# Fourier mixer of a two-block transformer kernel: projection folded into the feature tables, token transform in even and odd halves

## The reference, cut to what matters

```python
def fourier_mixer(hf, fnet_w, fnet_b):
    b, s, _ = hf.shape
    g = hf.reshape(b, s, FNET_GROUPS, FNET_GROUP_DIM).astype(jnp.float32)
    mixed = jnp.real(jnp.fft.fft2(g, axes=(1, 3), norm="ortho")).astype(hf.dtype)
    out = jnp.einsum('bsgc,gcd->bsgd', mixed, fnet_w) + fnet_b[None, None]
    return out.reshape(b, s, FNET_WIDTH)

def first_block(x, ...):
    x = x + 0.5 * swiglu(rms_norm(x, ffn1_norm), ffn1_w_gate, ffn1_w_up, ffn1_w_down)
    h = rms_norm(x, mix_norm)
    u = h @ w_in
    f_out = fourier_mixer(u[..., :o0], fnet_w, fnet_b)
    a_out = gqa_attention(u[..., o0:o1], u[..., o1:o2], u[..., o2:], q_norm, k_norm)
    x = x + jnp.concatenate([f_out, a_out], axis=-1) @ w_out
    ...
```

## Time and profile before

| what | value |
|---|---|
| median of 3 runs | 1262.18 us (1260.85 to 1262.86) |
| the profiled execution's own time | 1260.8 us |
| span of its trace | 1259.0 us |
| PE busy | 1243.9 us (99%) |
| PEld busy | 1104.9 us (88%) |
| DVE busy | 925.3 us (73%) |
| ACT busy | 657.5 us (52%) |
| mean granted TensorE clock | 0.995 |

### The profile page before, as it was taken

One profiled execution on the slowest core, in us unless ns is written; L12 is line 12 of the kernel. 1 busy time (PEld: TensorE's weight loads), 2 busy tenths in 40 slices (PEclk: granted clock), 3 DMA queues, 4 the chain that ended last, 5 costly groups with the idle time before them and its releaser, 6 DMA issues.

```text
span 1259.0 us, 18129 instructions
## 1 busy us (share of the span) xinstructions
PE 1243.9 (99%) x7458; PEld 1104.9 (88%) x7458; DVE 925.3 (73%) x1295; ACT 657.5 (52%) x867; POOL 30.9 (2%) x23
## 2 busy tenths in 40 slices
PE   8999999999999999999999999999999999999997
PEld 7888889878888888888888888889998888888886
DVE  7887856587877855988658777659977657877743
ACT  6655534364655543546546555545555445555432
POOL 0000000000000000440000000000000000000000
PEclk9999999999999999999999999999999999999998
DMA  8465754134555663555336555753435534555550
GB/s 312 174 227 186 230 190 164 68 106 163 200 179 189 200 235 128 173 197 173 136 137 228 201 179 190 226 176 135 168 135 182 186 134 139 200 197 192 192 185 34
DMA packets 51426, 221.74 MB, mean 176 GB/s; under 512 B 4464, under 2 KB 5776, under 8 KB 30864
## 3 DMA queue, kind: packets, MB, share of 16 engines
q1 hardware_dynamic: 51200, 220.52, 50.9%
q10 hardware_dynamic: 144, 0.07, 0.0%
HBM read 219.52 MB, written 1.05 MB: 175 GB/s over the span
## 4 chain that ended last, share of the span: by engine, by line
PE 91%; DVE 6%; ACT 1%; DMA 1%; issue 1%; SPq 0%; DVEq 0%; ACTq 0%
PE bank L405 48%; PE bank L435 21%; PE bank L409 7%; PE bank L426 4%; PE bank L474 2%; DVE wt L1153 2%; PE bank L685 2%; PE bank L713 2%; PE bank L451 1%; PE bank L477 1%; DVE xn L1162 1%; DVE x L1167 1%; PE bank L510 1%; DVE x L1168 1%; PE bank L456 1%; DMA x<-x_t 1%
## 5 line engine op out<-in xcount | busy, mean ns | idle before, releaser
L1153 DVE TENSOR_TENSOR wt<-raw,wt 128x2048 fp32r<-128x2048 f32 x202 | 464.1, 2299 | 69.0 <-ACT wt L831 68.6
L831 ACT ACTIVATE wt<-raw 128x2048 fp32r<-128x2048 f32 x202 | 385.9, 1911 | 125.4 <-PE bank L409 83.5
L405 PE MATMUL bank<-xn,wt 128*128 128x512 f32 x1712 | 417.3, 394 | 4.7 <-DVE xn L1162 4.1
L405 PEld LDWEIGHTS bank<-xn,wt 128*128 128x128 f32 x1712 | 314.1, 189 | 67.6 <-DVE xn L1162 6.7
L405 PE MATMUL bank<-h,wt 128*128 128x512 f32 (+1 forms) x1024 | 250.4, 393 | 0.0
L435 PEld LDWEIGHTS bank<-xn,wt 128*128 128x128 f32 x1856 | 239.3, 192 | 9.3
L435 PE MATMUL bank<-xn,wt 128*128 128x256 f32 x1856 | 242.9, 283 | 0.0
L405 PEld LDWEIGHTS bank<-h,wt 128*128 128x128 f32 (+1 forms) x1024 | 184.3, 188 | 35.7 <-issue 1.1
L1251 DVE TENSOR_TENSOR scratch<-bank,rest 128x512 f32<-128x512 f32 x98 | 67.6, 690 | 85.9 <-ACT rest L843 85.6
L906 ACT ACTIVATE h<-scratch 128x256 fp32r<-128x256 f32 x88 | 36.8, 418 | 158.8 <-DVE scratch L1291 158.8
L843 ACT ACTIVATE rest<-bank 128x512 f32<-128x512 f32 x114 | 67.6, 593 | 68.2 <-PE bank L435 67.9
(11 more groups left out here) (186 smaller groups left out, 961.6 us busy)
## 6 DMA issues: line engine op xcount, KB each, us to landing
raw<-weights SPq DMA_DIRECT2D x158, 1024.0 KB, 4.9
raw<-weights SPq DMA_DIRECT2D x88, 512.0 KB, 5.2
raw<-weights SPq DMA_DIRECT2D x8, 256.0 KB, 4.5
k_t<-mem_t SPq DMA_DIRECT2D x2, 1024.0 KB, 8.0
x<-x_t SPq DMA_DIRECT2D x4, 256.0 KB, 5.6
raw<-weights SPq DMA_DIRECT2D x8, 128.0 KB, 4.3
out_t<-work SPq DMA_DIRECT2D x4, 256.0 KB, 2.3
v_s<-fourier SPq DMA_DIRECT2D x2, 256.0 KB, 5.3
```

The lines of the kernel that those rows point to most:

```text
L405: return pe.matmul(out, hi, a.rearrange("p a s -> p (a s)"), start=first, stop=False, skip_group_check=True)
L831: act.activation(wt[t % RING][:, 0], raw[t % RING][:], ACT.Copy).then_inc(weight_hi, 1)
L1153: dve.tensor_tensor(wt[t % RING][:, 1], raw[t % RING][:], wt[t % RING][:, 0].bitcast(F32), ALU.subtract).then_inc(weight_lo, 1)
```

## The change

Three parts. **Tables**: in tiles 16 and 18 of `gu0`, after 4 of the tile's long matmuls, TensorE multiplies the cosine and the sine half of `dft_feature` by `f_w` of all four groups (`feature_table`, one float32 matmul of 512 columns each) into bank 6. ScalarE copies the products over the old tables (`table_out`), the first after its step of tile 17, the second after that of tile 19. **Token transform**: a group's feature products (now with the projection in them, 4 matmuls of 128 columns) are multiplied by the token tables for 129 and 128 of the 256 tokens alone, the cosine (even) and sine (odd) part in halves of a bank. ScalarE copies the even part (`even_copied`), VectorE makes the two halves of the tokens by a difference, written backwards, and a sum (`group_whole`). **Order**: the projection is gone; ScalarE's and VectorE's queues are written anew, `grouped_attention` waits for `f_whole` 3 behind `scores(0)` on TensorE and for `f_split` 4 on ScalarE.

```diff
+TABLES_AT = 16
...
+        seq = [bank[:, 2 * B + 1, :].rearrange("p (a s) -> p a s", a=2), acc[3]]
+        mixed_s = [scratch[:, 4 + g, :] for g in range(4)]
+
+        cos_table = [v_s[:, 0, P:2 * P]] + [v_s[:, 1, g * P:(g + 1) * P] for g in range(1, 4)]
+        sin_table = [f_w[:, g, :] for g in range(4)]
...
+            def feature_table(i):
+
+                pe.wait_ge(fourier_landed, FOURIER_DMAS)
+                if i:
+                    pe.wait_ge(table_copied, i)
+                pe.matmul(bank[:, 6, :], dft_feature[:, i * P:(i + 1) * P], f_w.rearrange("p g d -> p (g d)"), start=True,
+                          stop=True).then_inc(table_made, 1)
...
+                tables = {TABLES_AT + 2 * i: {2: lambda i=i: feature_table(i)} for i in range(2)} if n == 0 else {}
...
                 scores(0)
+                pe.wait_ge(f_whole, 3)
...
             gate_up(0, "x0")
+            pe.wait_ge(table_copied, 2)
...
                 for n in range(NT):
-                    mm = pe.matmul(feat[:, n, :], work[:, g, n * P:(n + 1) * P], dft_feature, start=True, stop=True)
+                    for i, table in enumerate((cos_table, sin_table)):
+                        mm = pe.matmul(feat[:, n, i * P:(i + 1) * P], work[:, g, n * P:(n + 1) * P], table[g], start=True, stop=True)
...
             for g in range(4):
-                f_s = probs[g % 2]
+                f_s, out = probs[g % 2], seq[g % 2]
                 pe.wait_ge(f_feat_copied, g + 1)
-                if g:
-                    pe.wait_ge(f_seq_copied, g)
+                if g == 1:
+                    pe.wait_ge(v_copied, 1)
+                if g > 1:
+                    pe.wait_ge(f_whole, g - 1)
                 for n in range(NT):
-                    pe.matmul(seq[:, 0, :], f_s[:, n, 0:P], dft_cos[:, n, :], start=n == 0, stop=False)
-                    mm = pe.matmul(seq[:, 0, :], f_s[:, n, P:2 * P], dft_sin[:, n, :], start=False, stop=n == NT - 1)
+                    pe.matmul(out[:, 0, 0:P + 1], f_s[:, n, 0:P], dft_cos[:, n, 0:P + 1], start=n == 0, stop=n == NT - 1)
+                for n in range(NT):
+                    mm = pe.matmul(out[:, 1, 0:P], f_s[:, n, P:2 * P], dft_sin[:, n, 0:P], start=n == 0, stop=n == NT - 1)
                 mm.then_inc(f_seq, 1)
                 if g < 3:
                     feature_sums(g + 1)
-                part("gqa", 0, ks=((2, 3), (3, 4), (4, 6), (6, 8))[g])
-                pe.wait_ge(f_seq_copied, g + 1)
...
-                pe.matmul(acc[3][:, 1, :], f_w[:, g, :], probs_t[g % 2][:, 0, :], start=True, stop=True).then_inc(f_out, 1)
+                    part("gqa", 0, ks=((2, 4), (4, 6), (6, 8))[g])
...
+                    if n == 0 and j in (TABLES_AT + 1, TABLES_AT + 3):
+                        table_out((j - TABLES_AT) // 2)
...
+            even_copied(0)
+            features_copied(1)
+            even_copied(1)
+            features_copied(2)
+            group_rounded(0)
+            even_copied(2)
+            features_copied(3)
+            after(FIRST["w_in"] + 4)
+            group_rounded(1)
+            even_copied(3)
+            group_rounded(2)
+            group_rounded(3)
...
+            def group_whole(g):
+
+                y, odd = mixed_s[g], seq[g % 2][:, 1, 1:P]
+                dve.wait_ge(f_even_copied, g + 1)
+                link(dve.tensor_tensor(y[:, S - 1:P:-1], y[:, 1:P], odd, ALU.subtract))
+                dve.tensor_tensor(y[:, 1:P], y[:, 1:P], odd, ALU.add).then_inc(f_whole, 1)
...
             head_rope(1)
+            group_whole(0)
+            group_whole(1)
             group_rest(0)
+            after(FIRST["w_in"] + 4)
+            group_whole(2)
             head_rope(2)
-            group_rest(1)
-            after(FIRST["w_in"] + 4)
-            group_rest(2)
-            group_rest(3)
+            group_whole(3)
+            for g in range(1, 4):
+                group_rest(g)
             grouped_attention()
```

More of the change, by code:

```diff
@@ L232, in program @@
         stat = acc[3]
-        feat, seq = (bank[:, 2 * B + i, :].rearrange("p (a s) -> p a s", a=2) for i in range(2))
+        feat = bank[:, 2 * B, :].rearrange("p (a s) -> p a s", a=2)
+        seq = [bank[:, 2 * B + 1, :].rearrange("p (a s) -> p a s", a=2), acc[3]]
+        mixed_s = [scratch[:, 4 + g, :] for g in range(4)]
+        cos_table = [v_s[:, 0, P:2 * P]] + [v_s[:, 1, g * P:(g + 1) * P] for g in range(1, 4)]
+        sin_table = [f_w[:, g, :] for g in range(4)]
         def pair_banks(name, j):
@@ L277, in program @@
         v_turned, v_copied = sem("v_turned"), sem("v_copied")
-        f_feat, f_feat_copied, f_seq, f_seq_copied, f_out, f_rounded, f_split = (
-            sem(n) for n in ("f_feat", "f_feat_copied", "f_seq", "f_seq_copied", "f_out", "f_rounded", "f_split"))
+        f_feat, f_feat_copied, f_seq, f_even_copied, f_whole, f_rounded, f_split = (
+            sem(n) for n in ("f_feat", "f_feat_copied", "f_seq", "f_even_copied", "f_whole", "f_rounded", "f_split"))
+        table_made, table_copied = sem("table_made"), sem("table_copied")
         a_scores, a_max, a_exp, a_probs, a_turned, a_turned_copied, a_out, a_rounded, a_split = (
@@ L542, in gate_up @@
                     square_tile(t0 + j, banks_for(phase, j), xn, ready=ready, in_parts=in_parts,
-                                beside=norm(name, n == 0).get(j, {}), ms=1 if j == FF - 1 and n < 2 else 2,
+                                beside={**norm(name, n == 0).get(j, {}), **tables.get(j, {})}, ms=1 if j == FF - 1 and n < 2 else 2,
                                 cuts=((2, 4, 6) if j == 0 else (4,)) if in_parts else (6,) if j == 0 else ())
@@ L759, in _ @@
                             beside={**norm("mix"), 3: {5: head_sums}, 4: {4: head_factors}}.get(j, {}))
-            pe.wait_ge(fourier_landed, FOURIER_DMAS)
             feature_sums(0)
@@ L888, in stream, with table_out @@
                         after(FIRST[write] + b)
+            def table_out(i):
+                act.wait_ge(table_made, i + 1)
+                if i == 0:
+                    act.activation(cos_table[0], bank[:, 6, 0:P], ACT.Copy)
+                    act.activation(v_s[:, 1, P:4 * P], bank[:, 6, P:4 * P], ACT.Copy).then_inc(table_copied, 1)
+                else:
+                    act.activation(f_w.rearrange("p g d -> p (g d)"), bank[:, 6, :], ACT.Copy).then_inc(table_copied, 1)
             def gate_up(n):
@@ L953, in grouped_attention @@
                 after(FIRST["gqa"])
+                act.wait_ge(f_split, 4)
                 for p in range(4):
@@ L1060, in _, with even_copied, group_rounded @@
             act.activation(v_s[:, :, 0:P], acc[3][:, 0, :].rearrange("p (t d) -> p t d", t=NT), ACT.Copy).then_inc(v_copied, 1)
-            for g in range(4):
+            def even_copied(g):
                 act.wait_ge(f_seq, g + 1)
[L1063 to L1070, removed]
-                    after(FIRST["w_in"] + 4)
+                act.activation(mixed_s[g][:, 0:P + 1], seq[g % 2][:, 0, 0:P + 1], ACT.Copy).then_inc(f_even_copied, 1)
+            def group_rounded(g):
+                act.wait_ge(f_whole, g + 1)
+                act.activation(h[:, g, 0, :], mixed_s[g], ACT.Identity, bias=v("fnet_b", g)).then_inc(f_rounded, 1)
+            even_copied(0)
[10 more added lines that the diff above has]
+            group_rounded(3)
             rest_part("gqa", 0)
```

2 lines of the change are left out of this document (1 added, 1 removed).

## The result

The changed kernel takes 1267.41 us (median of 6 runs, 1265.02 to 1268.69) beside 1261.51 for the kernel before (6 runs, 1258.48 to 1262.86). The ratio is 1.0053, 95% interval 1.0043 to 1.0064: it is slower, by 0.5%. The forecast was 1268.0 (1264.6 to 1270.8), slower with a chance of 0.87. The profiled execution took 1266.89 us, its span is 1265.1 against 1259.0, and its mean granted clock 0.992 against 0.995.

A forecast was written before the change was run, and what follows sets the result against it. TensorE was taken to bound the kernel. Tables +1.7, wait in tile 18 +4.9, clock +1.5 and mixer -2.4 gave +5.7 us, from a median of 1262.2 to 1268.0 us, range 1264.6 to 1270.8.

The forecast's parts named there:

- What bounds: Whole kernel: TensorE, at work 1243.9 of 1259.0 us, so its time is the kernel's unless another engine takes over.
- The tables: In `gu0`: four matmul passes of 512 columns on TensorE, not hidden, +1.7 us (0.9 to 2.0).
- The wait in tile 18: In `gu0`: TensorE waits at the second table for ScalarE's copy of the first, +4.9 us.
- The clock behind it: After tile 18's wait: TensorE's granted clock falls, +1.5 us, ends nothing and 2.7.
- the head sums: Two-column matmuls in `w_in`, half clock behind them, 1.5 us lost: the row the clock's price was taken from.
- The dearer end: Upper end for the clock behind tile 18's wait: as at the program's start, 0.229 us a matmul, 2.7 us lost.
- rival 1: Tile 18 of `gu0`: the wait is there but the clock does not fall, +4.2, 1266.4 us; chance 0.17.
- The mixer: Mixer to attention start: TensorE saves 4.7 us, but VectorE reaches the first maxima only 2.4 us earlier, so -2.4.
- The sum: Whole kernel: tables, wait, clock and mixer together +5.7 us, median 1268.0 us, slower.
- 3 and 4: Rivals: 3, the wait costs nothing, -0.7 us, chance 0.08; 4, TensorE's saved columns arrive whole, 3.0 us gained, chance 0.05.
- rival 3: Tile 18's wait costs nothing while VectorE limits the mixer: -0.7, 1261.5 us, no visible difference; chance 0.08.
- Rival 2: The clock falls a second time, at the 2.2 us wait before the transposes: +7.0, 1269.2 us; chance 0.18.

The follow-up runs named there:

- mixer_order: Against early_table: VectorE's mixer queue reordered, split of `gqa` 1 in its first gap, one rest less ahead of the maxima; 1256.51 us, ratio 0.9974.
- filled_wait: Against the changed kernel: five useless float32 matmuls of 512 columns ahead of the wait in tile 18; 1264.33 us, ratio 1.0031 to the kernel before.
- table_late: Against the changed kernel: tables made in tiles 16 and 19, copied out after ScalarE's steps of 17 and 20; 1264.30 us, ratio 1.0028.
- mixer_alone: Against early_table: no tables made or copied, unprojected tables used in the same shapes, values wrong; 1257.60 us, ratio 0.9978 to the kernel before.
- early_table: Against the changed kernel: first table made in tile 15, one tile earlier, the second still in 18; 1259.67 us, ratio 0.9997 to the kernel before.
- change_again: The changed kernel measured once more, nothing altered; 1268.69 us, ratio 1.0054 to the kernel before.
- order_again: mixer_order measured once more, nothing altered; 1259.73 us, ratio 0.9984 to the kernel before.

## Why the prediction was right

- **What bounds**: right. The waits put on TensorE came out as time (4.83 and 2.82 us, each with half clock behind), and the one taken away by mixer_order as gain.
- **The tables**, 1.7: 1.76 in the trace (0.88 each), 2.1 by runs.
- **The wait in tile 18**, 4.9: 4.83 idle, the table 5.0 us late. The copy was expected 5.9 us into tile 18 and is there; filled_wait and table_late confirm that its place follows from ScalarE's queue alone.
- **The clock behind it**, 1.5, between 0 and 2.7: the mechanism was right (filled_wait takes the idle time away, and the clock stays up). The size is 1.6 us in one execution, as said, and 3.0 in another, beyond the range's end; the runs' 2.8 holds other falls too. So the term is the least certain of the sum, and too small if anything. I took the head sums because their low activity was most alike; the low clock behind them in the earlier trace rows is the shorter of two lengths that the later traces show. The dearer end, 2.7, came near 3.0 by luck: it was read from the warm-up, for which the profile records a granted clock of 1.00, so no row shows that its 0.229 us a matmul was such a fall. The Trainium skill's rule that a wait between bursts of matmuls lets the next burst start cold ("TensorE: Matmul & The Clock Gate", section "HAM oscillation — how this bites in real kernels") holds here: the burst behind the 4.83 us started at 0.50, so rival 1, no fall, was wrong in both traces.
- **The mixer**, -2.4 of -4.7: -2.9 in the trace, -2.8 by runs (mixer_alone). TensorE's columns were priced right (1.79 a group, 1.85 said), and so was the cut by VectorE: the wait of 1.98 before the transposes (2.2 said). VectorE came to the maxima 0.5 us earlier than added up: 0.2 of it stands ahead of the split, which starts 9.11 us behind the mixer's start and not 9.33, and the rest is prices a little too high (the third rotation 2.70 for 2.8, the pairs of halves 0.53 for 0.65 and 0.6). The backward write costs as much as the forward one, 0.28 and 0.29.
- **The sum**, +5.7: +5.9 by the medians, +0.53% or 6.7 us by the ratio. The clock term was 0.1 too small in one trace and 1.5 in the other, the tables 0.1, the wait's delay 0.1 (5.0 for 4.9); the mixer's gain was 0.5 too small, which pulls the other way. So the total is nearer than its parts, and that is luck. (The terms add to 1267.9 on the median; 1268.0 is a rounding.) The profiled pair's 6.1 us hides an exchange of two clock falls of about 1.5 us each.
- **Rivals**: 3 and 4 needed ScalarE ahead of its queue; early_table shows what rival 3 described, no measurable difference once the wait is gone. Rival 2 appeared in one trace of an experiment (mixer_alone), not in the two of the changed kernel.

mixer_order, the change with the table a tile earlier and VectorE's gap used, is faster than both kernels, than the one before by 0.2 to 0.3%: 0.9974 and 0.9984 of its time in two sets, both intervals below 1.

## What to carry to other kernels

When a matmul reads or overwrites what a slower engine must first copy, find that copy in the engine's queue and count to the instruction ahead of it: the step named for tile 17 ends 5.9 us into tile 18, and one tile's distance decided over 7 us, more than the change could gain. Price idle time on a saturated TensorE at its length, and a wait of several us at a fall of the clock beside it: here the clock fell behind 4.83 us in both traces (1.6 and 3.0 us lost) and behind 2.82 us in the one (1.7 lost), but behind 1.98 us in one of six. And when columns are saved on TensorE, look at who is due next on the other engines: here idle gaps of 2.1 us earlier in VectorE's queue were what had to be filled for the saving to arrive.

## What the runs showed of the hardware that I had not expected

- The same few-column stretch lets the clock fall in one execution and not in the next, of the same kernel too: the head sums are followed by half clock in seven of the ten kept traces (4.92 us for 28 matmuls in the kernel before, 3.43 in the first execution of the changed one, while its second, change_again, has the fall).
- At the head sums, the sums ahead of the convolution and the waits discussed here, the granted clock was at 0.50 for 3.4 us or for 6.8, and for nothing between (behind the wait in tile 18, 3.4 in one execution and 6.8 in another of the same kernel).
- So the runs of one kernel lie in groups by their mean granted clock. In order_again five runs with 0.995 to 0.997 took 1255.6 to 1256.9 us and six with 0.991 to 0.994 took 1259.7 to 1261.4, and the median fell into the upper group by one run. Means over many runs, or distances inside the trace, told differences of 2 us; medians of 9 to 11 runs did not.
